# Two changes to a two-block forward pass: raw x is transposed beside the output product of block 2, and two totals in the down stage stand one product later

## The reference, cut to what matters

```python
mod = (silu(c) @ w_ada + b_ada)            # 24 pieces of 512 columns, also called totals
x = x + g1 * (mixed @ w_out)               # the output product
hl2 = rmsnorm(x, norm2_w) * (1.0 + sc2) + sh2
x = x + g2 * (square(relu(hl2 @ w_mlp1)) @ w_mlp2)
return rmsnorm(x, final_norm_w)
```

## Time and profile before

| | |
|---|---|
| median of 3 runs | 3586.29 us (3581.09 to 3593.0) |
| the profiled execution, its own time | 3589.1 us |
| its span | 3587.3 us |
| PE busy | 3455.7 us, 96% |
| DVE busy | 2357.0 us, 66% |
| ACT busy | 1610.5 us, 45% |
| mean granted clock of PE | 0.982 |
| moved by transfers | 687.84 MB, 192 GB/s |

### The profile page before, as it was taken

One profiled execution on the slowest core, in us unless ns is written; L12 is line 12 of the kernel. 1 busy time (PEld: TensorE's weight loads), 2 busy tenths in 40 slices (PEclk: granted clock), 3 DMA queues, 4 the chain that ended last, 5 costly groups with the idle time before them and its releaser, 6 DMA issues.

```text
span 3587.3 us, 42873 instructions
## 1 busy us (share of the span) xinstructions
PE 3455.7 (96%) x15838; PEld 2819.1 (79%) x15838; DVE 2357.0 (66%) x2911; ACT 1610.5 (45%) x2107; POOL 33.4 (1%) x28
## 2 busy tenths in 40 slices
PE   7999999999999999999999999999878899999998
PEld 6888888887778888888888887878535788888887
DVE  5667888888666666777776663566665665656565
ACT  5555555555334545555554442444212343434343
POOL 0000000000000000000000000000000000000000
PEclk9999999999999999999999999999998999999999
DMA  7557777776667466777777753466003466666664
GB/s 236 155 176 219 228 224 221 226 228 209 217 216 213 143 185 218 230 231 230 229 227 250 250 180 96 149 194 199 1 0 106 143 221 200 222 200 218 203 219 158
DMA packets 357809, 687.84 MB, mean 192 GB/s; under 512 B 24591, under 2 KB 28704, under 8 KB 356384
## 3 DMA queue, kind: packets, MB, share of 16 engines
q1 hardware_dynamic: 357664, 685.82, 60.9%
HBM read 683.64 MB, written 2.10 MB: 191 GB/s over the span
## 4 chain that ended last, share of the span: by engine, by line
PE 67%; issue 21%; DVE 6%; DMA 2%; ACT 2%; DVEq 2%; SPq 0%; ACTq 0%; POOL 0%; POOLq 0%
PE acc L2048 16%; PE acc L2050 16%; PE acc L2049 16%; PE acc L2324 4%; PE acc L2326 4%; PE acc L2325 4%; DMA w_raw<-in_w_down 2%; DVE w_lo L1228 2%; PE turn L2255 1%; DVE ada_sum L1331 1%; PE acc L2588 1%; PE turn L2069 1%; DVEq L1323 1%; PE side L2061 1%; ACT w_hi L768 1%
## 5 line engine op out<-in xcount | busy, mean ns | idle before, releaser
L1228 DVE TENSOR_TENSOR w_lo<-w_raw,w_hi 128x1024 fp32r<-128x1024 f32 x708 | 839.1, 1221 | 394.0 <-ACT w_hi L768 360.3
L768 ACT ACTIVATE w_hi<-w_raw 128x1024 fp32r<-128x1024 f32 x708 | 739.4, 1062 | 731.9 <-DMA w_raw<-in_w_up 315.5
L2048 PE MATMUL acc<-w_hi,in_h 128*128 128x512 f32 x1408 | 552.7, 393 | 0.0
L2050 PE MATMUL acc<-w_hi,in_l 128*128 128x512 f32 x1408 | 548.6, 390 | 0.0
L2049 PE MATMUL acc<-w_lo,in_h 128*128 128x512 f32 x1408 | 548.1, 389 | 0.0
L1987 DVE TENSOR_TENSOR w_lo<-w_raw,w_hi 128x1024 fp32r<-128x1024 f32 x252 | 302.6, 1222 | 205.8 <-ACT w_hi L1192 198.1
L1192 ACT ACTIVATE w_hi<-w_raw 128x1024 fp32r<-128x1024 f32 x252 | 264.6, 1060 | 337.4 <-DMA w_raw<-in_w_mlp 336.5
L2324 PE MATMUL acc<-w_hi,in_h 128*128 128x512 f32 x992 | 395.8, 399 | 14.7 <-issue 5.8
L2326 PE MATMUL acc<-w_hi,in_l 128*128 128x512 f32 x992 | 390.6, 394 | 0.0
L2325 PE MATMUL acc<-w_lo,in_h 128*128 128x512 f32 x992 | 390.4, 394 | 0.0
L1331 DVE SCALAR_TENSOR_TENSOR ada_sum<-w_raw,silu_c,ada_sum 128x512 f32<-128x512 f32 x450 | 327.5, 750 | 31.4 <-issue 7.5
(11 more groups left out here) (347 smaller groups left out, 4730.6 us busy)
## 6 DMA issues: line engine op xcount, KB each, us to landing
w_raw<-in_w_up SPq DMA_DIRECT2D x352, 512.0 KB, 3.7
w_raw<-in_w_mlp SPq DMA_DIRECT2D x256, 512.0 KB, 3.7
w_raw<-in_w_in SPq DMA_DIRECT2D x200, 512.0 KB, 3.7
w_raw<-in_w_ada SPq DMA_DIRECT2D x192, 512.0 KB, 4.2
w_raw<-in_w_down SPq DMA_DIRECT2D x176, 512.0 KB, 4.6
w_raw<-in_w_o SPq DMA_DIRECT2D x64, 512.0 KB, 3.7
w_raw<-in_w_out SPq DMA_DIRECT2D x32, 512.0 KB, 3.7
x_sb<-in_x SPq DMA_DIRECT2D x1, 2048.0 KB, 7.9
```

The lines of the kernel that those rows point to most:

```text
L768: nc.scalar.activation(hi[s][:, ks], raw[s][:, ks], ACT.Copy).then_inc(w_hi[s][h], 1)
L1228: nc.vector.tensor_tensor(lo[s][:, ks], raw[s][:, ks], hi[s][:, ks].bitcast(F32), ALU.subtract).then_inc(w_lo[s][h], 1)
L2048: nc.tensor.matmul(acc[p][i][:], high(kt)[:, tok], hi[s][:, k], start=(kt == first), stop=False)
L2050: last = nc.tensor.matmul(acc[p][i][:], low(kt)[:, tok], hi[s][:, k], start=False, stop=(kt == final))
```

## The change

There are three edits in one kernel.

1. **x is turned raw.** After products 7, 9 and 13 of the output product (two after a chunk's last), and once more after product 15, PE transposes the finished chunk of `x_sb` against the identity, 8 transposes each (`turn_added`). ACT copies them out of PSUM with the feature's scale into a new fp32 buffer `n2_f` (`scaled_chunk`, 4 copies of 128 by 256 each). When the root is known, DVE still writes it on the diagonal; PE multiplies a matrix of ones with the two diagonal tiles (2 matmuls into bank `side[0]`, use "root"), which gives each token's root on all partitions. DVE multiplies `n2_f` by that (8 of 128 by 512), ACT adds the shift and rounds to `in_h` (16 of 128 by 256), DVE makes `in_l` from `n2_f`, shift and `in_h` (16 of 128 by 256). The 8 diagonal units of `turn_normed` go. Each of the MLP's first four products waits for its own four 128-row steps of `in_l`, no longer for all.
2. **Totals one product later.** (1, 4) and (2, 4) of `DN_TOTAL` become (1, 5) and (2, 5), in both layers.
3. **The wait at block 2's start** for `ada_mod` moves from before its first product to `running_sums`, where `side[0]` is first used.

```diff
-    DN_TOTAL = {(0, 0): 5, (1, 4): 6, (2, 4): 7, (3, 8): 8}
+    DN_TOTAL = {(0, 0): 5, (1, 5): 6, (2, 5): 7, (3, 8): 8}
...
+        def scaled_chunk(c):
+            for u in (2 * c, 2 * c + 1):
+                b, k = UNITS["n2", u]
+                act_.wait_ge(t_full[b], k)
+                for f in range(2):
+                    kt = 2 * u + f
+                    a = nc.scalar.activation(n2_f[:, kt], tb[b][:, f * TOK:(f + 1) * TOK], ACT.Copy, scale=scale2[:, 2, kt:kt + 1])
+                a.then_inc(t_free[b], 1)
+
         for n in range(16):
             if n >= 2:
                 split_hi2(OUT0 + n + 2)
             if n in OUT_LAST:
                 x_squares2(OUT_LAST.index(n) + 1, OUT_LAST.index(n))
-        whole_hi([("n2", i) for i in range(8)], in_f, in_h, 0)
+            if n - 3 in OUT_LAST:
+                scaled_chunk(OUT_LAST.index(n - 3))
+        scaled_chunk(3)
+        for i in range(8):
+            act_.wait_ge(n2_s, i + 1)
+            for kt in (2 * i, 2 * i + 1):
+                a = nc.scalar.activation(in_h[:, kt], n2_f[:, kt], ACT.Identity, bias=mod[:, 48 + kt, 0:1])
+            a.then_inc(part2_hi, 1)
...
-        whole([("n2", i) for i in range(8)], in_f, in_l, in_h, 2, lambda kt: mod[:, 48 + kt, 0:1], 0, 24)
+        def block_n2_low(i):
+            dve.wait_ge(part2_hi, 24 + i + 1)
+            for kt in (2 * i, 2 * i + 1):
+                a = nc.vector.scalar_tensor_tensor(in_l[:, kt], n2_f[:, kt], mod[:, 48 + kt, 0:1], in_h[:, kt].bitcast(F32), ALU.add, ALU.subtract)
+            a.then_inc(part2_lo, 1)
+
+        for u in (6, 7):
+            b, k = UNITS["n2", u]
+            dve.wait_ge(t_free[b], k + 1)
+        dve.wait_ge(side_full[0], SIDE[0]["root"] + 1)
+        for i in range(8):
+            two = n2_f[:, 2 * i:2 * i + 2]
+            nc.vector.tensor_tensor(two, two, side[0][:, 0:TOK].unsqueeze(1).to_broadcast([P, 2, TOK]), ALU.mult).then_inc(n2_s, 1)
+            if i > 0:
+                block_n2_low(i - 1)
+        block_n2_low(7)
...
-        pe.wait_ge(ada_mod, 2 * ADA_LAYER + 1)
         for j in range(12):
...
+        def turn_added(c):
+            pe.wait_ge(x_up, c + 1)
+            for u in (2 * c, 2 * c + 1):
+                turn2(("n2", u), [x_sb[:, j, kt * P:(kt + 1) * P] for kt in (2 * u, 2 * u + 1) for j in range(TT)])
+
...
             product2(OUT0 + n, 4 * k, [(c % 2, in_h, in_l, CH)], 0, 4 * OUT[OUT_FIRST[c]][1], 4 * OUT[OUT_LAST[c]][1] + 3)
+            if n - 2 in OUT_LAST:
+                turn_added(OUT_LAST.index(n - 2))
+        turn_added(3)
+        o = fill_side(0, "root")
         pe.wait_ge(diag_s, 1)
-        turn_normed("n2", x_sb)
-        pe.wait_ge(part2_lo, 24)
+        for i in range(TT):
+            last = nc.tensor.matmul(o[:, i * P:(i + 1) * P], masks[:, ONES], diag[:, i], start=True, stop=True)
+        last.then_inc(side_full[0], 1)
...
                 for s in range(NS):
+                    if c == 0:
+                        pe.wait_ge(part2_lo, 16 + 2 * s + 2)
                     product2(mlp_product(NS * c + s), 4 * s, [(p, in_h, in_l, CH)], q)
```

More of the change, by code:

```diff
@@ L255, in program @@
     hid_l = sbt("hid_l", [P, KT, TOK], F32R, at(48))
+    n2_f = sbt("n2_f", [P, KT, TOK], at=at(32))
     y2 = [sbt(f"y2_{i}", [P, TT, CH], at=at(88 + 4 * i)) for i in range(2)]
@@ L309, in program @@
     yf_s, conv_s, gdiag_s = sem("yf_s"), sem("conv_s"), sem("gdiag_s")
+    n2_s = sem("n2_s")
     hid_hi, hid_sq, final_s = sem("hid_hi"), sem("hid_sq"), sem("final_s")
@@ L532, in program @@
         side_uses[b] += [("norm", o) for o in range(2)] + [("conv", o, c) for o in range(2) for c in range(2)]
+        side_uses[b] += (["root"], [])[b]
     SIDE = [{u: k for k, u in enumerate(side_uses[b])} for b in range(2)]
@@ L2377, in fill_side @@
             return side[b]
[L2379 to L2383, removed]
         def turn_x2(u):
@@ L2409, in running_sums @@
             o = fill_side(0, "cum")
+            pe.wait_ge(ada_mod, 2 * ADA_LAYER + 1)
             pe.wait_ge(da_s, 1)
```

## The result

| | before | after |
|---|---|---|
| median of the runs, first measurement | 3586.87 us (6 runs, 3581.09 to 3593.0) | 3569.23 us (6 runs, 3562.14 to 3575.23) |
| ratio, 95% interval | | 0.9949 (0.9937 to 0.9962) |
| median, repeated with the last experiments | 3586.13 us (10 runs) | 3566.33 us (6 runs, 3563.28 to 3567.72) |
| ratio, 95% interval | | 0.9944 (0.9930 to 0.9957) |
| span of the profiled execution | 3587.3 us | 3573.4 us |

The account below looks back on a forecast made before the run. PE, busy 96% of the span, was taken to bound the kernel. Terms 2.6 + 7.5 + 2.1 + 6.7 + 0.1 = 19.0 us off the 3586.3 median gave 3567.3 us, range 3557 to 3580.

Parts of the forecast that it names:

- Totals, chunk 1 of layer 0: Layer 0's down stage, chunk 1: the total no longer waits, but a later load does; 2.6 us gained, bounds 0 and 7.4.
- The walk along the ring: Layer 0, chunk 1: following loads, rounding and DVE's work through the weight pieces; PE stands 3.2 us at piece 9's second half.
- less about 1.6 for the slow stretch behind such an idle: Layer 0, chunk 1: deduction from 4.2 us for 8 matmuls running 0.2 us slower after the wait at piece 9.
- Chunk 2: Layer 0's down stage: a wait of 7.45 us becomes 2.9 us on w_lo at piece 5; 7.5 us gained, bounds 5.5 and 9.
- The rival that waits take the totals' place: Layer 0, both chunks: DVE or the loads set the pace, the total's wait becoming other waits; 9.5 us gained, 3577; chance 0.14.
- Layer 1: Layer 1's down stage: the waits of 0.91 and 1.24 us before the totals go; 2.1 us gained, bounds 1 and 2.3.
- Passage: Output product to block 2's MLP: MLP starts 10.5 us earlier, less 3.0 for transposes and 0.8 slow stretch; net 6.7 us.
- The rule on transposes and the clock: Passage to the MLP: by the skill's rule alone, the MLP opens slow for longer and the passage term is 6.3 us.
- Block 2's start: Block 2's first product still waits for DVE's last addition, so moving the modulation wait gains 0.1 us, not 2.8.
- The copies on ACT hold up no weight: Rival in the output product: ACT's copies wait for PE's transposes and delay weights; slower, 3603 us; chance 0.05.
- The MLP does not open late: Rival at the passage: broadcast source costs as much again, DVE's chain grows 5 us, the term falls to 1; 3573; chance 0.09.
- the rival that all is kept: Rival over the whole change: loads land sooner, no slow stretch after short idles; 27 us gained, 3559; chance 0.13.

Follow-up runs that it names:

- e7_warm: Kernel after with fp32 matmuls of no use in PE's idle time of the passage to the MLP; single time 3564.79 us.
- e2: Kernel after with the old table of totals, (1,4) and (2,4), so the passage change without moved totals; 3580.13 us, ratio to before 0.9984.
- e5: Kernel after with only chunk 1's total moved, (1,5), and chunk 2's back at (2,4); 5.5 us earlier than before at layer 1's first matmul on the keys.
- e6_chunk2: Kernel after with only chunk 2's total moved, (2,5), chunk 1's back at (1,4); 5.2 us earlier than before at layer 1's first matmul on the keys.
- e4_startwait: Kernel after with PE's wait for the modulation put back before block 2's first product; one time, 3565.49 us.
- e3_allwait: Kernel after, but the MLP's first product waits for all 16 rows of the low part, as before; 3572.89 us.
- e11: Kernel after with nine fp32 matmuls of no use in PE's idle times of block 2's filter stage; 3564.69 us, ratio to before 0.9936.
- e10: Kernel after with chunk 2's modulation pieces spread wider, useless matmuls in passage and filter stage, DVE's y_sum memsets moved ahead; 3556.62 us, ratio to before 0.9918.
- e1: Kernel before with only the table of totals changed to (1,5) and (2,5); 3569.25 us, ratio to before 0.9953.

## Why the prediction was right, point by point

The median came 1.9 us from the forecast, 3569.23 for 3567.3. That is nearer than the measurement can tell: six single times lie over 13 us, and the second median is 3566.33. By the stretches the gain is 20.2 us, for 19.0: chunk 1's term was 2.0 us too small, chunk 2's 0.8 too large, the others right to 0.2. The prediction also calls PE's idle stretches few; there are 46 of them, 118 us together, and the change touches a handful.

- **Totals, chunk 1 of layer 0: forecast 2.6 us, measured 4.6 by the stretches (4.0 in the pair of before and after).** The walk along the ring held: the stand came at piece 9's second half (until 941.80, forecast 942.7), and with the one at piece 10 it is 1.63 + 1.43 = 3.06 us, forecast 3.2. The term that was wrong is "less about 1.6 for the slow stretch behind such an idle"; without it the working gives 4.2. It was not wrong because short idle times leave the clock alone. In e7_warm, whose code is the same here, the clock was lost behind the first wait:

```profile
941.08 0.50 PE L2083 MATMUL acc<-w_hi,ah 128*128 128x512 f32 x1 [1.86 <-DVE w_lo L1247]
...
942.46 0.63 PE L2085 MATMUL acc<-w_hi,al 128*128 128x512 f32 x1
```

The matmuls lost 1.7 us to the lower clock, the wait at piece 10 was gone, and A is 66.9 us all the same. Piece 10's low part, behind a modulation sum on DVE, sets the end here, and a slow stretch at piece 9 only uses up the wait for it. That second stand the prediction did not foresee.

- **Chunk 2: forecast 7.5, measured 6.7 (7.3 in the pair).** The stall of 2.9 us on `w_lo` came with 3.01, its slow stretch of 1.5 us with 7 matmuls at 0.2 more, 1.4 us. That the pair agrees so well is in part luck: before's profile lost 2.9 us to slow matmuls behind the old total where e2 and e5 lost 1.7 and 2.3, and the new stretch lost 0 to 2.8 us in other profiles. The rival that waits take the totals' place was half right here: they do, for 3 of 7.45 us.
- **Layer 1: forecast 2.1, measured 2.3 (2.5 in the pair).** The two waits of 0.91 and 1.24 us are gone, and the totals take 0.95 in place of 1.02. That both waits count alike, 0.91 + 1.24, was wrong: by e5_chunk1 and e6_chunk2, one profile each, the second total carries all of it that shows.
- **Passage: forecast 6.7 (of it 10.5 earlier, 3.0 and 0.8 back), measured 6.7.** From the last output matmul to the first of the MLP 11.98 us, not 22.15: 10.2 earlier. The 3.95 us from DVE's start to the second low part, for which the prediction shows no working, came as 4.17 (2833.15 to 2837.32). The output product is 2.5 us longer (69.63 for 67.12), so 8 transposes cost 0.84 and not 1.03 there. The stretch from the MLP's first matmul to the last of all is 1.0 us longer (722.23 for 721.27), of which 0.22 is the wait at the third piece, the "no stall, but no slack" of the prediction. Ten matmuls were slow, where 13 were forecast and before had 9. That the parts are each off by some tenths and the sum exact is luck.
- **The rule on transposes and the clock.** By the Trainium skill, "TensorE: Matmul & The Clock Gate", Part 4, with transposes not counting as busy the term would have been 6.3. Ten matmuls were slow, fewer than the 15 of that reading and than the 13 of the sum by rows. No run here took the transposes away from before the MLP, so the rule itself is not tested; that fp32 matmuls in the same gaps end the slow opening (e7_warm) agrees with it and does not prove it.
- **Block 2's start: forecast 0.1, measured nothing** (2.82 us idle before, 2.80 after, and C no longer in e4_startwait).
- **Rivals.** The copies on ACT hold up no weight: the one wait of PE in the output product, 3.22 us at the start of D, is the same in both kernels. The MLP does not open late, since the broadcast source costs nothing extra. In chunk 1 the rival that all is kept was right in after's profile in one thing, that no slow stretch follows the short idle times; e7_warm shows that this isn't always so, and that it costs nothing at that place.

## What to carry to other kernels

Where a small product waits for a sum on another engine, moving it one step later removes the wait only up to the next thing that is late; look at once at who is in front of that on the same engine (here DVE's modulation sums before a low part), and spread it: here that gave another 5.5 us. Two such moves in a row have to be tried together: the first alone can lengthen the second wait. In a passage between two stages look at the granularity of the first wait before the order of the work: here the new order gave nothing without it (e3_allwait), while the waits alone would have given 3.5 us at most by my estimate, not tested. A slow opening of TensorE is not worth curing while the next input is late by as much: here it took both cures to win 3.0 us. And since the same wait of 3.0 us cost nothing in slow matmuls in one profile and 2.8 us in another, such a cost should be read from several profiles.

## What was unexpected

The stretch of block 2's filter stage, the same instructions in all kernels but e11 and e10, takes 72.2, 73.6 to 73.9, 80.3 or 82.2 us in twelve profiles, with nothing between, at a mean granted clock of 0.88, 0.86, 0.79 and 0.77. In the profile of after the clock is at its lower level for much of 2590.96 to 2607.00 (0.54), right behind an idle time of 1.38 us that is in before's profile too. There a window as long, from the same matmul, has it at the higher level, and 37 matmuls in it where after has 20:

```profile
2602.17:2618.20 16.03, 16.03 (x37) 1.00 0.00 0
```

PE's timing up to that point is the same in both: 2591.96 - 2562.27 = 29.69 us and 2580.74 - 2551.06 = 29.68, then 10.21 and 10.22 to the next group. So what PE did in this stage up to that point does not tell the two apart. The Trainium skill, "TensorE: Matmul & The Clock Gate", Part 1, says that the number of slow matmuls at a kernel's start varies from run to run of the same kernel; the rows agree and show it in the middle of one, at 8 to 10 us a time. Of the stretches outside A to D it varies most, by 10.0 us; from B's end to C's start it is 5.3 us between the profiles, from C's end to the filter stage 4.6, from the Fourier products to D 4.4 (near 122.6 in eight profiles, near 126.4 in six). So it is probably the largest source of the 12 us and more over which the times of one kernel scatter, and it is more than any single part of this change is worth. The medians of 4 to 10 runs could not have ranked e1 to e3, and e4 has one run; stretches between fixed matmuls did, to 0.6 us in D and 0.9 in C, but only to 1.5 and 2.8 in A and B.
